# Sums of squares of the gated-delta heads from rounded squares and remainders, in a two-block transformer kernel on one core

## The reference

```python
def l2norm(x):
    return x * lax.rsqrt(jnp.sum(x * x, axis=-1, keepdims=True) + EPS)

qkv = jax.nn.silu(causal_short_conv(jnp.concatenate([gq, gk, gv], axis=-1), conv_w))
cq, ck, cv = jnp.split(qkv, [GDN_WIDTH_K, 2 * GDN_WIDTH_K], axis=-1)
...
q_g = l2norm(cq.reshape(B, S, GDN_QK_HEADS, GDN_DK)) * GDN_DK ** -0.5
k_g = l2norm(ck.reshape(B, S, GDN_QK_HEADS, GDN_DK))
...
o_g = gated_delta_chunked(...)   # chunks of 64 tokens, S = a (I - beta k k^T) S + beta k v^T
```

## Time and profile before

| | us |
|---|---|
| median of 3 runs | 1381.51 |
| lowest, highest | 1381.33, 1381.86 |
| the profiled execution, whole | 1381.49 |
| its span in the trace | 1379.8 |
| PE busy | 1362.9 |
| VectorE busy | 1025.1 |
| ScalarE busy | 802.3 |

### The profile page before, as it was taken

The page is one execution under the profiler, slowest core; times in us unless marked ns, Lnnn a source line. Parts: engine busy times, 40 slices in busy tenths (PEclk is TensorE's granted clock), DMA queues, the critical chain, the costliest instruction groups (busy, mean ns, idle before and its releaser), DMA issues.

```text
span 1379.8 us, 25257 instructions
## 1 busy us (share of the span) xinstructions
PE 1362.9 (99%) x9092; PEld 1237.9 (90%) x9092; DVE 1025.1 (74%) x1601; ACT 802.3 (58%) x1310; POOL 23.4 (2%) x71
## 2 busy tenths in 40 slices
PE   8999999999999999999999999999999999999998
PEld 8999999988888888888899999999999898888887
DVE  5786786677666686666788888888888877666665
ACT  4444554644433354444678898898898844544443
POOL 6000000000000000000000000000000000000000
PEclk9999999999999999999999999999999999999999
DMA  8574555555555746665574453554544276566661
GB/s 265 151 192 141 149 143 168 186 183 197 199 184 184 221 132 208 198 186 183 153 188 127 129 149 102 145 144 116 136 128 126 87 186 212 158 207 197 197 187 61
DMA packets 298383, 227.82 MB, mean 165 GB/s; under 512 B 10882, under 2 KB 280404, under 8 KB 298324
## 3 DMA queue, kind: packets, MB, share of 16 engines
q1 hardware_dynamic: 298324, 227.01, 55.3%
HBM read 225.90 MB, written 1.08 MB: 165 GB/s over the span
## 4 chain that ended last, share of the span: by engine, by line
PE 96%; DVE 2%; ACT 1%; DVEq 0%; issue 0%; POOL 0%; ACTq 0%; POOLq 0%
PE G L1974 9%; PE G L1976 9%; PE G L1975 9%; PE M L1979 7%; PE M L1991 7%; PE M L1980 7%; PE G L1991 7%; PE M L1981 7%; PE G L1993 4%; PE M L1993 4%; PE G L2718 2%; PE G L1979 2%; PE G L1981 2%; PE G L1980 2%; PE G L2094 2%; PE M L2540 1%
## 5 line engine op out<-in xcount | busy, mean ns | idle before, releaser
L1156 DVE TENSOR_TENSOR w_lo<-w_raw,w_hi 128x2048 fp32r<-128x2048 f32 (+2 forms) x249 | 481.1, 1936 | 155.3 <-ACT w_hi L624 151.1
L624 ACT ACTIVATE w_hi<-w_raw 128x2048 fp32r<-128x2048 f32 x198 | 377.9, 1909 | 173.6 <-PE G L1976 75.3
L1974 PE MATMUL G<-xa,w_hi 128*128 128x256 f32 x992 | 292.9, 295 | 0.0
L1976 PE MATMUL G<-xa,w_lo 128*128 128x256 f32 x992 | 280.5, 283 | 0.0
L1975 PE MATMUL G<-xa,w_hi 128*128 128x256 f32 x992 | 280.3, 283 | 0.0
L1974 PEld LDWEIGHTS G<-xa,w_hi 128*128 128x128 f32 x992 | 189.5, 191 | 1.9 <-DVE w_lo L1156 0.7
L1975 PEld LDWEIGHTS G<-xa,w_hi 128*128 128x128 f32 x992 | 189.6, 191 | 0.0
L1976 PEld LDWEIGHTS G<-xa,w_lo 128*128 128x128 f32 x992 | 189.2, 191 | 0.0
L1979 PE MATMUL M<-w_hi,xb 128*128 128x512 f32 x304 | 119.0, 392 | 0.6 <-DVE xb L1156 0.5
L1980 PE MATMUL M<-w_lo,xb 128*128 128x512 f32 x304 | 118.7, 391 | 0.0
L1981 PE MATMUL M<-w_hi,xb 128*128 128x512 f32 x304 | 118.3, 389 | 0.0
(11 more groups left out here) (405 smaller groups left out, 2515.6 us busy)
## 6 DMA issues: line engine op xcount, KB each, us to landing
w_raw<-in_w_in SPq DMA_DIRECT2D x150, 512.0 KB, 4.9
w_raw<-in_ffn_w_in SPq DMA_DIRECT2D x88, 512.0 KB, 5.1
w_raw<-in_w_ff SPq DMA_DIRECT2D x64, 512.0 KB, 4.3
w_raw<-in_ffn_w_out SPq DMA_DIRECT2D x44, 512.0 KB, 4.8
w_raw<-in_w_in SPq DMA_DIRECT2D x33, 256.0 KB, 3.2
w_raw<-in_w_out SPq DMA_DIRECT2D x16, 512.0 KB, 4.1
w_raw<-in_w_branch_gdn SPq DMA_DIRECT2D x16, 512.0 KB, 5.2
w_raw<-in_w_branch SPq DMA_DIRECT2D x12, 512.0 KB, 4.2
```

What stands on the lines that cost most here:

```text
L624: nc.scalar.activation(w_hi[:, slot, :], w_raw[:, slot, :], ACT.Copy).then_inc(hi_ready, 1)
L1156: return v.tensor_tensor(dst, src, hi.bitcast(F32), ALU.subtract)
L1974: mm(out_, w[0], x[0], start=first, stop=False)
L1976: return mm(out_, w[1], x[0], start=False, stop=last_)
```

## The change

Four edits in the stage "heads". ScalarE squares q and k twice: into eg in float32 as before, and into sq_hi in the rounded format (in xb_hi[:, 13:15]); the signal sqh_ready stands behind the second. VectorE subtracts (low_of, eg - sq_hi) into sq_lo, between the half w_low and the two scalings of vn1, and signals sql_ready. PE replaces the float32 product by two rounded products by ones_r into the same bank: the first at the old place, the second behind quarter 15 in the middle heads and behind the turns in the first head. The Exp of the forget projection moves on ScalarE from before token_rstd to behind it, and the clamp on VectorE from before the gate to behind it. The rest of the diff merges semaphores (wi_done and cum_done into forget_done, ab_done and gsum_done into decay_done, gate2_tanh into gate_tanh) and leaves the waits where they were.

```diff
+    sq_hi, sq_lo = (part[:, 13:15, :].rearrange("p k t -> p (k t)") for part in (xb_hi, xb_lo))
...
-                nc.scalar.activation(eg[:, 0:2 * T], acc[:, 0:2, :].rearrange("p n t -> p (n t)"), ACT.Square).then_inc(sq_ready, 1)
+                nc.scalar.activation(eg[:, 0:2 * T], acc[:, 0:2, :].rearrange("p n t -> p (n t)"), ACT.Square)
+                nc.scalar.activation(sq_hi, acc[:, 0:2, :].rearrange("p n t -> p (n t)"), ACT.Square).then_inc(sqh_ready, 1)
             log_exp_set()
-            if gemm:
-                nc.scalar.activation(eh, G[:, 1, T:2 * T], ACT.Exp, scale=-1.0).then_inc(evac[1], 1)
             if main:
                 act.wait_ge(hpv_done, i)
                 token_rstd(hrs.rearrange("p (i c) -> p i c", i=TT), M[:, 1, 0:T].rearrange("p (i c) -> p i c", i=TT),
                            h_sum, h_rstd, QSCALE).then_inc(hrs_ready, 1)
+            if gemm:
+                nc.scalar.activation(eh, G[:, 1, T:2 * T], ACT.Exp, scale=-1.0).then_inc(evac[1], 1)
             split_j(2)
...
             if gemm:
                 w_low_half(c0 + 1 + RING, 1, i, 6)
+                dve.wait_ge(sqh_ready, i + 1)
+                low_of(sq_lo, eg[:, 0:2 * T], sq_hi).then_inc(sql_ready, 1)
...
+            if main and gemm:
+                hgrn_gate(i)
             if gemm:
                 dve.wait_ge(evac[1], EV_HEADS[1] + 2 + i * 3)
                 v.tensor_scalar(eh, eh, 2.0 ** 62, None, ALU.min).then_inc(eh_ready, 1)
-            if main and gemm:
-                hgrn_gate(i)
-            if gemm:
                 v.tensor_copy(yi, ident[:].unsqueeze(1).unsqueeze(1).to_broadcast([P, TT, 2, P]))
...
-                pe.wait_ge(sq_ready, i + 1)
-                mm(M[:, 2, :], ones[:], eg[:, 0:2 * T], start=True, stop=True).then_inc(ss_done, 1)
+                pe.wait_ge(sqh_ready, i + 1)
+                mm(M[:, 2, :], ones_r, sq_hi, start=True, stop=False)
...
             if main:
                 quarter(15)
+            if gemm:
+                pe.wait_ge(sql_ready, i + 1)
+                mm(M[:, 2, :], ones_r, sq_lo, start=False, stop=True).then_inc(ss_done, 1)
             if main and gemm:
                 hgrn_turned()
```

More of the change, by code:

```diff
@@ L293, in emit @@
     dots_done, relu_ready, relu_used = sem("dots_done"), sem("relu_ready"), sem("relu_used")
-    forget_step, fln_ready, cum_done = (sem(n) for n in ("forget_step", "fln_ready", "cum_done"))
+    forget_step, fln_ready, forget_done = (sem(n) for n in ("forget_step", "fln_ready", "forget_done"))
     va_ready = sem("va_ready")
-    wi_done, decay_step, ab_done = sem("wi_done"), sem("decay_step"), sem("ab_done")
+    decay_step, decay_done = sem("decay_step"), sem("decay_done")
     c_turned_step, ck_loaded, mck_ready = sem("c_turned_step"), sem("ck_loaded"), sem("mck_ready")
@@ L318, in emit @@
     vecs_loaded, vec_done, vec_ready = (sem(n) for n in ("vecs_loaded", "vec_done", "vec_ready"))
-    abln_ready, gsum_done, lb_exp = (sem(n) for n in ("abln_ready", "gsum_done", "lb_exp"))
+    abln_ready, lb_exp = (sem(n) for n in ("abln_ready", "lb_exp"))
     hpv_done, hsq_ready, hss_done, hrs_ready, hfin, lt2_ready, qk_ready = (
@@ L334, in emit @@
                          "ntc_ready"))
+    sqh_ready, sql_ready = sem("sqh_ready"), sem("sql_ready")
     vn0_done, vn0_ready, cross_done, r1_ready, vn1_done, vn1_ready, go_done = (
@@ L338, in emit @@
         sem(n) for n in ("gsq_ready", "gss_done", "grs_ready", "ogh_ready", "ogl_ready"))
-    gate_tanh, gate2_tanh = sem("gate_tanh"), sem("gate2_tanh")
+    gate_tanh = sem("gate_tanh")
     ohh_ready, ohl_ready, ym_ready, ymh_ready, yml_ready = (
@@ L1045, in head @@
                 own = gates2[:, ds(i - 1, 1), :, :].rearrange("p n b t -> p (n b t)")
-                nc.scalar.activation(own, own, ACT.Tanh, scale=0.5).then_inc(gate2_tanh, 1)
+                nc.scalar.activation(own, own, ACT.Tanh, scale=0.5).then_inc(gate_tanh, 1)
                 act.wait_ge(wl_ready, i * 8)
@@ L1207, in _ @@
         qi_copy(0)
-        dve.wait_ge(wi_done, 1)
+        dve.wait_ge(forget_done, 1)
         v.tensor_copy(wi, M[:, 4, 0:TT * SMALL].rearrange("p (i h) -> p i h", i=TT))
@@ L1243, in _ @@
         add_scores(0)
-        dve.wait_ge(cum_done, 1)
+        dve.wait_ge(forget_done, 2)
         v.tensor_copy(c_f, M[:, 5, 0:TT * NH].rearrange("p (i h) -> p i h", i=TT)).then_inc(c_turned_step, 1)
         qi_copy(2)
-        dve.wait_ge(cum_done, 2)
+        dve.wait_ge(forget_done, 3)
         v.tensor_copy(c_turned[0:TT * NH, :], M[0:TT * NH, 5, P:2 * P]).then_inc(c_turned_step, 1)
@@ L1621, in _ @@
         w_low(FIRST["ba"] + RING)
-        dve.wait_ge(ab_done, 1)
+        dve.wait_ge(decay_done, 1)
         v.tensor_copy(abx, M[:, 5, 0:4 * VH].rearrange("p (i h) -> p i h", i=TT))
@@ L1820, in head @@
             if not main:
-                dve.wait_ge(gsum_done, 1)
+                dve.wait_ge(decay_done, 2)
                 sums = M[:, 4, 0:3 * VH].rearrange("p (i h e) -> p i h e", i=3, e=2)
@@ L1930, in sum_low @@
             low_of(xa_lo[:, 2 * u:2 * u + 2, :], o_h[:, 2 * u:2 * u + 2, :], xa_hi[:, 2 * u:2 * u + 2, :]).then_inc(yml_ready, 1)
-        dve.wait_ge(gate2_tanh, GH)
+        dve.wait_ge(gate_tanh, 6 + GH)
         for n in range(4):
@@ L2180, in _ @@
                                       ident[0:SMALL, 0:SMALL])
-        ins.then_inc(wi_done, 1)
+        ins.then_inc(forget_done, 1)
         static_chunk(2, col_gemm)
@@ L2188, in _ @@
         mm(M[:, 5, NH:2 * NH], ones[:], log_f[:, 0, :], start=True, stop=False)
-        mm(M[:, 5, NH:2 * NH], tri[:], log_f[:, 1, :], start=False, stop=True).then_inc(cum_done, 1)
+        mm(M[:, 5, NH:2 * NH], tri[:], log_f[:, 1, :], start=False, stop=True).then_inc(forget_done, 1)
         static_chunk(3, col_gemm)
@@ L2192, in _ @@
         pe.wait_ge(c_turned_step, 1)
-        nc.tensor.transpose(M[0:TT * NH, 5, P:2 * P], c_f.rearrange("p i h -> p (i h)"), ident[:]).then_inc(cum_done, 1)
+        nc.tensor.transpose(M[0:TT * NH, 5, P:2 * P], c_f.rearrange("p i h -> p (i h)"), ident[:]).then_inc(forget_done, 1)
         static_chunk(4, col_gemm)
@@ L2397, in ab_turned @@
                                           ident[0:2 * VH, 0:2 * VH])
-            ins.then_inc(ab_done, 1)
+            ins.then_inc(decay_done, 1)
         def sums_of_g():
@@ L2403, in sums_of_g @@
                 mm(M[:, 4, VH * b:VH * b + VH], tri[:], gdec[:, b, :], start=True, stop=True)
-            mm(M[:, 4, 2 * VH:3 * VH], ones[:], gdec[:, 0, :], start=True, stop=True).then_inc(gsum_done, 1)
+            mm(M[:, 4, 2 * VH:3 * VH], ones[:], gdec[:, 0, :], start=True, stop=True).then_inc(decay_done, 1)
         c0 = FIRST["heads"]
```

## The result

The changed kernel takes 1384.65 us as a median of 13 runs (lowest 1384.37, highest 1385.03), against 1381.51 us for the kernel before (lowest 1381.32, highest 1381.86, 13 runs). The ratio is 1.0023 with a 95% interval of 1.0015 to 1.0030: 3.1 us slower, where 1384.9 was forecast. The profiled execution has a span of 1382.9 us, 3.1 more than before.

What follows compares the result with a forecast made beforehand. ScalarE's list from line 936 to the copy of the turned v was taken as the bound in that third of each middle head, PE from there on. Seven heads x 0.54 less 0.40 gave +3.4, 1384.9 us, range 1383.3 to 1387.5.

Steps and rivals of the forecast that it cites:

- PE's saving: Line 2648's float32 product (0.86 us) replaced by two rounded ones (0.46): PE's list 0.40 us shorter in each of eight heads.
- The second Square: ScalarE's added 128x512 Square lengthens its list up to the copy of line 1083 by 0.54 us, bounds 0.48 and 0.65.
- The copy sets PE's arrival in bank M0: PE waits for ScalarE's copy of the turned v (line 1083); its loss there grows from 0.11 to about 1.05 us.
- The small edits: Moved Exp neutral for ScalarE's total, subtraction fits VectorE's list, a likely 0.1 to 0.2 us wait at line 2626 swallowed.
- Sum: Seven heads at +0.54 us and the first head at -0.40 together give +3.4 us, or 1384.9.
- Rival (a): PE does not wait for the line 1083 copy; PE's list alone counts, 8 x 0.40 off, 1378.3 us; 6%.
- Rival (b): Unmarked slack in ScalarE's list covers its extra work; PE keeps only the first head's saving, -0.4, 1381.1 us; 12%.
- Rival (c): VectorE's list after line 1865 delivers the inverse's start late; up to 4.8 us on top, 1389.7 us; 10%.

Runs made afterwards that it cites:

- PE's part alone: Kernel before, with ScalarE squaring once into the rounded tile and PE forming two rounded products from it, no subtraction: 1380.90 us against 1381.29.
- the last pair: VectorE's second half w_low of chunk 3 moved behind its token copy, in the changed and the VectorE-rounding kernel, both with finished-head copy late: 1386.28 and 1382.79 us.

## Why the prediction was right

The time: 1384.9 was forecast with a range of 1383.3 to 1387.5, and 1384.65 was measured. By its own steps:

**PE's saving.** 0.40 us a head. The first head shows 0.39 (1.76 to 1.37), and the growth of the wait with PE's part alone shows 0.39 a trip.

**The second Square.** 0.54 us from start to start was read from line 1067, and the record after has 0.54. As an effect on the time it was 0.51 and 0.56 for the first and second extra Square. The estimate by the Trainium skill (ScalarE: Activation LUTs, "What ACT_TABLE_LOAD costs") was 0.52, 0.02 below the record.

**The copy sets PE's arrival in bank M0.** The wait grew from 0.26 to 1.14 us a trip, where about 1.2 was forecast, and the loss from 0.11 to 0.99, where 1.05 was. The list up to the copy grew by 0.53. The trip grew to 50.67 us, forecast 50.65.

**The small edits.** The Exp, the subtraction and the wait of 0.1 to 0.2 us ahead of line 2626 (measured 1.3 / 7 = 0.19) were held to be free. The two runs that undo the first two say so, and with the Exp back the third grew to 0.46 without a change in time.

**Sum.** 7 x 0.54 - 0.40 = +3.4 against a measured +3.1, whose interval of 1.0015 to 1.0030 is 2.1 to 4.1 us.

**What was incomplete.** The prediction took the copy for the one place where ScalarE's list ends in a wait of PE, and from the copy on it took PE itself for the bound. It wrote that VectorE's list from line 1865 on shifts by the same 0.54 and that the margins in the rest stay as they are. That is true, and it kept the sum right, since both ends came later by the same amount. But PE was not alone in setting the rest of the trip. The margin was about 0: PE's first step of the inverse already followed VectorE's line 1913 at the least distance, with no mark in the view of waits. My later expectations took 0.3 us there, from the turns of line 2694 alone, and forecast 1382.1 and 1378.6 where 1384.49 and 1381.08 came out. A sum for a slowdown doesn't notice a second end of the same list; a sum for a gain does. One small reading was off too: besides the pauses that the prediction names, ScalarE has one of 0.07 us ahead of line 1067, which the change leaves in place.

Rival (a), PE's list alone, is refuted by PE's part alone. Rival (b), a hidden margin, is refuted by the equal steps of one and two Squares. Rival (c), something late behind the copy by VectorE's work, didn't occur: without the subtraction the time is the same, and VectorE idles 0.92 us before the w_low at 814.87, where it idled 0.86 before the change. But its 10% was given with a margin in mind that wasn't there: any delay beyond the 0.54 us would have counted in full.

## What to carry to other kernels

PE at 99% was paced here by ScalarE at 58%. In such a kernel take the stretch where the edit lies, find what the busy engine waits for last, however short, and follow its releaser back: a wait by which PE lost only 0.11 us meant here that the releaser's list had no margin. Work moved from the busy engine to that list cost its full length each trip, and the saving was lost in the wait. The place for it was an engine that idles there: on VectorE it cost nothing that could be measured. Before forecasting a gain from shortening such a list, look for every place where it ends, those without a wait in the profile too: the load of the first step of the inverse started 0.11 or 0.12 us behind VectorE's record in all twelve kernels ahead of the last pair, whether a wait was marked or not, and 0.5 us behind it in the last two.
